# Last level of a blocked triangular inverse: 64x64 masked products against 32x32 blocks

## The reference, cut to what matters

```python
def rwkv7_scan(r, w, k, v, kk, a, s0):
    def step(s, inp):
        rt, wt, kt, vt, kkt, at = inp
        sa = jnp.einsum('nbhij,nbhj->nbhi', s, kkt)
        s = (s * wt[..., None, :] - sa[..., :, None] * (kkt * at)[..., None, :]
             + vt[..., :, None] * kt[..., None, :])
        return s, jnp.einsum('nbhij,nbhj->nbhi', s, rt)
```

## Time and profile before

| | us |
|---|---|
| median of 3 runs | 5243.85 |
| profiled execution | 5262.38 |
| its span | 5260.8 |
| stages ahead of the scans | 0 to 1540 |
| scans | 1540 to 3232 |
| readout, experts, combine | 3232 to 5261 |

### The profile page before, as it was taken

One profiled execution on the slowest core, in us unless ns is written; L12 is line 12 of the kernel. 1 busy time (PEld: TensorE's weight loads), 2 busy tenths in 40 slices (PEclk: granted clock), 3 DMA queues, 4 the chain that ended last, 5 costly groups with the idle time before them and its releaser, 6 DMA issues. The chain is left out here.

```text
span 5260.8 us, 122702 instructions
## 1 busy us (share of the span) xinstructions
PE 4374.7 (83%) x47298; PEld 2979.5 (57%) x47298; DVE 2214.8 (42%) x4008; ACT 1249.5 (24%) x3133; POOL 1565.5 (30%) x1949
## 2 busy tenths in 40 slices
PE   3998799989968988888888886788499999988990
PEld 1877676666648777777877775444133333333330
DVE  1112166666645454554544544888211111111118
ACT  0001044344423333333323332332000000000002
POOL 0000001001025464554545543443322222221224
PEclk7999999999989999999999988888699999999995
DMA  9311165556442223232232324442675888899766
GB/s 310 124 59 68 58 198 186 166 173 197 150 128 68 77 71 91 71 78 68 71 91 71 89 57 122 144 138 97 232 299 209 341 350 341 362 373 400 316 265 263
DMA packets 365528, 916.96 MB, mean 174 GB/s; under 512 B 181136, under 2 KB 220432, under 8 KB 332080
## 3 DMA queue, kind: packets, MB, share of 16 engines
q1 hardware_dynamic: 310224, 759.97, 41.4%
q0 software_dynamic: 47392, 133.02, 7.2%
q10 hardware_dynamic: 7488, 17.83, 0.9%
HBM read 951.09 MB, written 211.26 MB: 221 GB/s over the span
## 5 line engine op out<-in xcount | busy, mean ns | idle before, releaser
L2410 PE MATMUL exp_gate_up<-exp_w_gate,exp_rows_and_rowsT 128*64 128x512 f32 x1664 | 768.2, 620 | 88.8 <-DMA exp_w_up<-in_moe_w_up_dram 87.9
L2410 PE MATMUL exp_gate_up<-exp_w_up,exp_rows_and_rowsT 128*64 128x512 f32 x1664 | 768.9, 621 | 0.0
L2410 PEld LDWEIGHTS exp_gate_up<-exp_w_gate,exp_rows_and_rowsT 128*64 128x64 f32 x1664 | 234.9, 143 | 588.6 <-issue 588.6
L1544 POOL TENSOR_TENSOR rw_A_level<-rw_A_rho_beta,const_level_masks 128x256 f32<-128x256 f32 x432 | 338.2, 799 | 706.6 <-DVE rw_A_rho_beta L1560 440.0
L721 PE MATMUL rwp_product<-rwp_hT,rwp_w_rw 128*128 128x256 f32 (+1 forms) x2016 | 445.0, 384 | 0.0
L874 PE MATMUL hgp_product<-hgp_hT,const_w_hg 128*128 128x256 f32 x1728 | 411.1, 394 | 26.5 <-DMA hgp_hT<-s_hT 15.7
L2362 DVE TENSOR_TENSOR exp_hidden<-exp_hidden,exp_gate_up 64x512 f32<-64x512 f32 x104 | 71.9, 692 | 821.4 <-ACT exp_hidden L2343 821.4
L721 PEld LDWEIGHTS rwp_product<-rwp_hT,rwp_w_rw 128*128 128x128 f32 (+1 forms) x2016 | 381.7, 190 | 61.6
L874 PEld LDWEIGHTS hgp_product<-hgp_hT,const_w_hg 128*128 128x128 f32 x1728 | 338.0, 199 | 87.9 <-DMA hgp_hT<-s_hT 16.1
L2434 PE MATMUL exp_down<-exp_w_down,exp_hiddenT 128*64 128x512 f32 x1664 | 380.0, 598 | 1.1
L1575 DVE TENSOR_TENSOR rw_inverse<-rw_inverse,rw_inverse_bank 128x512 f32<-128x512 f32 x288 | 195.8, 684 | 349.6 <-PE rw_inverse_bank L1454 347.6
(11 more groups left out here) (384 smaller groups left out, 7977.6 us busy)
## 6 DMA issues: line engine op xcount, KB each, us to landing
exp_w_gate<-in_moe_w_gate_dram SPq DMA_DIRECT2D x104, 2048.0 KB
exp_w_up<-in_moe_w_up_dram SPq DMA_DIRECT2D x104, 2048.0 KB
exp_w_down<-in_moe_w_down_dram SPq DMA_DIRECT2D x104, 2048.0 KB
s_rw_in<-prep_operands SPq DMA_DIRECT2D x72, 514.0 KB, 4.0
rw_operands<-s_rw_in SPq DMA_DIRECT2D x72, 514.0 KB, 5.6
rw_tokens<-s_rw_tm SPq DMA_DIRECT2D x144, 192.0 KB, 6.5
hg_qkf<-s_hg_in SPq DMA_DIRECT2D x36, 768.0 KB, 7.9
mod_w<-in_w_mod_dram SPq DMA_DIRECT2D x24, 1024.0 KB, 26.1
```

The costliest lines, as they stand in the source:

```text
L1544: nc.gpsimd.tensor_tensor(self.al[d][l % 2][:], self.ar[u][d][:, :, 0, :], self.K["lvc"][:, d, l, :].unsqueeze(1).broadcast_to([P, NPAIR, ...
L2410: i = nc.tensor.matmul(pgu[u][q:q + BLK], xT[:, k, r * BLK:(r + 1) * BLK], w[r][:, k, :], start=(k == 0), stop=(k == KD - 1))
```

## The change

Level 5 joins the two diagonal blocks of 32. All that is new in the inverse is one block of 32x32 for each head, and its inputs are one block of 32x32 of the masked Gram product and the two diagonal blocks. For direction 0 the rows and columns 0 to 31 count as solved and 32 to 63 as the rest, for direction 1 the other way round (`halves`). After the change:
- cross5 multiplies 32x32 blocks, with the left operand taken from `rw_A_rho_beta` itself. It no longer waits for `level_ready`.
- ScalarE copies half of the columns of X at level 5 (all 128 partitions).
- grow5 multiplies 32x32 blocks.
- VectorE copies the new block into the inverse with two instructions of 32 partitions in place of the addition; one for each head of the pairs, the second with the semaphore.
- GpSimd makes no mask product for level 5. The counts of `level_ready` go from 6 to 5 a step, and the product of level 1 waits for cross3 of the step before, where it waited for cross5.

```diff
+    def halves(self, d):
+        early, late = slice(0, RW_C // 2), slice(RW_C // 2, RW_C)
+        return (early, late) if d == 0 else (late, early)
...
-            pe.wait_ge(s["level_ready"], 6 * n + l + 1)
+            if l < 5:
+                pe.wait_ge(s["level_ready"], 5 * n + l + 1)
             pe.sem_inc(self.turns, 1)
+            if l == 5:
+                solved, rest = self.halves(d)
+                for j in range(NPAIR):
+                    for h in (0, RW_C):
+                        i = nc.tensor.matmul(self.pa[d][at(rest, h), 0, j, solved], self.ar[u][d][at(solved, h), j, 0, rest],
+                                             self.rt[u][d][at(solved, h), 1, j, solved], start=True, stop=True)
+                i.then_inc(s["x_psum"], 1)
+                return
...
+            if l == 5:
+                solved, rest = self.halves(d)
+                for j in range(NPAIR):
+                    for h in (0, RW_C):
+                        i = nc.tensor.matmul(self.pa[d][at(solved, h), 0, j, rest], self.x[d][at(rest, h), j, solved],
+                                             self.rt[u][d][at(rest, h), 0, j, rest], start=True, stop=True)
+                i.then_inc(s["rd_psum"], 1)
+                return
...
-            nc.scalar.activation(self.x[d][:], self.pa[d][:, 0], ACT.Copy).then_inc(s["x_ready"], 1)
+            some = self.halves(d)[0] if l == 5 else slice(0, RW_C)
+            nc.scalar.activation(self.x[d][:, :, some], self.pa[d][:, 0, :, some], ACT.Copy).then_inc(s["x_ready"], 1)
...
-        for l in range(6):
+        for l in range(5):
...
-                    wait(pool, s["x_psum"], 5 * n + {0: -1, 1: 0, 3: 1, 4: 2, 5: 3}[l])
+                    wait(pool, s["x_psum"], 5 * n + {0: -1, 1: -2, 3: 1, 4: 2}[l])
...
-                    V.tensor_tensor(rt[:, 0], rt[:, 0], self.pa[d][:, 0], ALU.add).then_inc(s["r_ready"], 1)
+                    solved, rest = self.halves(d)
+                    V.tensor_copy(rt[solved, 0, :, rest], self.pa[d][solved, 0, :, rest])
+                    second = slice(RW_C + solved.start, RW_C + solved.stop)
+                    V.tensor_copy(rt[second, 0, :, rest], self.pa[d][second, 0, :, rest]).then_inc(s["r_ready"], 1)
```

More of the change, by code:

```diff
@@ L1449, in grow @@
             pe.sem_inc(self.turns, 1)
+            if l == 5:
[6 more added lines that the diff above has]
+                return
             for j, q in heads:
                 i = nc.tensor.matmul(self.pa[d][q, 0, j, :], self.x[d][q, j, :], self.rt[u][d][q, 0, j, :], start=True, stop=True)
-            if l < 5:
-                for j, q in heads:
-                    i = nc.tensor.matmul(self.pa[d][q, 1, j, :], self.rt[u][d][q, 0, j, :], self.x[d][q, j, :], start=True, stop=True)
+            for j, q in heads:
+                i = nc.tensor.matmul(self.pa[d][q, 1, j, :], self.rt[u][d][q, 0, j, :], self.x[d][q, j, :], start=True, stop=True)
             i.then_inc(s["rd_psum"], 1)
         chain = {"rhs": rhs, "solve": solve, "out": out, "state": state}
+        at = lambda part, h: slice(h + part.start, h + part.stop)
         if chain_only:
@@ L1532, in pool @@
         nc = self.nc
-        for l in range(6):
+        for l in range(5):
             for d in range(2):
                 s = self.s[d]
-                yield (({0: 3.1, 1: 5.1, 2: 7.1, 3: 10.1, 4: 16.1, 5: 22.1}[l] + d) / (2 * len(RW_ORDER)))
+                yield (({0: 3.1, 1: 5.1, 2: 7.1, 3: 10.1, 4: 16.1}[l] + d) / (2 * len(RW_ORDER)))
                 if l == 0:
@@ L1556, in mask @@
             if k == 0:
-                wait(dve, s["level_ready"], 6 * n)
+                wait(dve, s["level_ready"], 5 * n)
             wait(dve, s["y_psum"], n - 1)
@@ L1566, in inverse @@
             if l == 0:
-                dve.wait_ge(s["level_ready"], 6 * n + 1)
+                dve.wait_ge(s["level_ready"], 5 * n + 1)
                 wait(dve, s["u_psum"], n - 1)
```

## The result

The changed kernel takes 5361.55 us (median of 4 runs, 5355.20 to 5361.73), the one before on the same chip 5243.45 us (4 runs). The ratio is 1.0213, with an interval of 1.0176 to 1.0250: slower by 118 us. 5248 was forecast, with 5278 as the top of the range.

What follows compares the result with a forecast made beforehand. The scan stage was taken to go by TensorE's order of blocks plus 211 us idle. Long steps -8 and clock +12 gave +4 us: 5248, no change, own range 5238 to 5254; 8 in 10: 5226 to 5278.

Steps and rivals of the forecast that it cites:

- Block cost: A cross5 or grow5 block of one direction on TensorE: 0.26 us instead of 0.47, by the slope from 128 to 64 columns.
- The rival that blocks don't get shorter: 32 columns take the 29 ns of 64, leaving only idle edits, within 2 us of 5244; chance 0.10.
- Short steps: 18 scan steps ending in cross5, grow5, two HGRN blocks: no gain, 0.84 us saved only lengthens gram0's wait for loads.
- Long steps: 18 steps ending in cross5, grow5, score block, HGRN's output: three blocks save 0.63 us each step; 8 us taken.
- stops swallow half of the savings: TensorE's "issue" stops make half of the long steps lose their 0.63 us, leaving 5.7 of 11.3 us.
- Copies, X, relaxed wait: VectorE's two copies, ScalarE's half copy of X, GpSimd's earlier level 1 product: hidden behind other work or waits, 0.
- GpSimd's products: 72 level masks fewer on GpSimd, 57.5 us of its 872: 0, since no TensorE wait names them.
- The clock: Idle time between cross5 and grow5 in long steps drops TensorE to 1.2 GHz: +12 us, at 8 a stretch.
- the slower rival: Four more long steps fall to 1.2 GHz between cross5 and grow5, through HGRN's output: +24 us, 5268; chance 0.33.

Runs made afterwards that it cites:

- The copies alone: The kernel before with only VectorE's last addition replaced by two copies of the new block; ratio 1.0016.
- the stricter wait: The change with 64x64 blocks and GpSimd's level 1 product waiting again for cross5 of the step before; ratio 1.0070 to the kernel before.
- full tiles with 32 columns: The change with cross5 and grow5 as 64x64 tiles fed 32 columns each, four matmuls per direction and product; ratio 1.0189 to the kernel before.
- quarter tiles with 128 columns: The change with every 32x32 block of cross5 and grow5 fed 128 columns instead of 32; ratio 1.0124 to the kernel before.

## Why the prediction was wrong
**Block cost (0.26 us): right in size, not in its reason.** Measured 0.265. The rival that blocks don't get shorter falls. But the slope by columns, from which the 0.26 came, isn't what made them shorter: a 64x64 tile with half the columns isn't faster (1.13 against 1.15 us for 32 records), a 32x32 tile is. To that extent the number was luck. The Trainium skill gives a floor of about 25 ns from start to start ("TensorE: Matmul & The Clock Gate", Part 1). Counted by record, as the prediction did, the trace does not agree for the quarter tile, 0.53 us / 32 = 17 ns a record; the full tile's 35 ns lie above the floor. Counted by matmul, of which each leaves two records, both lie above it.

**Short steps (no gain): roughly right.** gram0's waits for loads were to grow from 31 to 45 us; they are 34.8. Short steps got 0.38 us shorter, so less of the 0.84 us went into these waits than was forecast.

**Long steps (-8): not seen.** The wait before cross5 of direction 1 grew from 0.82 to 0.92 us, where 1.0 was forecast. But the only long step of after without a long fall, the first one profiled, takes 51.20 us where the same step before takes 49.69; that is one step, with 3 us at the low clock. That stops swallow half of the savings has no run for or against it.

**Copies, X, relaxed wait (0): right.** The copies alone give 1.0016, the copies with the half copy of X and the product kept 1.0009, and the stricter wait gives nothing back. A copy takes 0.28 us (0.25 taken), X 0.28 us (0.38 before):

```profile
L1600 DVE COPY rw_inverse<-rw_inverse_bank 32x128 f32<-32x128 f32 x72 | 20.2, 280 | 72.9 <-PE rw_inverse_bank L1467 71.8
...
L1526 ACT ACTIVATE rw_X<-rw_inverse_bank 128x128 f32<-128x128 f32 x72 | 20.0, 278 | 108.6 <-PE rw_inverse_bank L1451 107.7
```

**GpSimd's products (0, "no wait on TensorE names it"): wrong.** Without them, and with the waits that go with them changed, the kernel is 0.5 per cent slower, some 25 us, with longer stops that the profile puts down to issue and some 25 us more at 1.2 GHz.

**The clock (+12): this step failed.** The place, the cause and the price of a fall were named, the sign was given (a stage clock of 0.93 or below; it is 0.87), and the slower rival is the mechanism that was shown. What failed is the count: "one or two further long stretches", four in the rival, where 16 of 17 long steps have a fall of 13.7 us or more and 3 had one before. 8 us a stretch was about right (6.6 by the estimate above). The count rested on one step with 2.58 us of work in 3.40 us that was held to have room, and on busy time: 0.2 us a block was taken out. The full tiles with 32 columns show that a block whose busy time is unchanged can lose the clock, so what the change took away isn't measured by its 0.84 us of busy time. By the measured sizes: 14.8 us more at 1.2 GHz in each of 17 long steps, at 0.89 / 2, cost 112 us, where 12 was taken.

## What to carry to other kernels
Before making matmuls smaller in front of a stretch that runs at the full clock, look at how near the clock's falls already are. Here 7 of 17 like steps fell at this place before, and all of them after; a few falls among like steps are a reason to put the whole number of such steps into the range, not one or two. Don't judge what is left in front of such a stretch by busy time alone: here two kernels with the same busy time there differed by 1.3 per cent. A saving at such a place cost about ten times itself (6.6 us a step, the estimate above, for the 0.63 us of three shorter blocks). And an experiment that added instructions to TensorE also added stops; widening a matmul did not.

## What the runs showed of the hardware
- Two blocks of 64x64 tiles took 1.13 us with 32 columns and 1.15 us with 64; 32x32 tiles took 0.53 us with 32 columns and 1.54 us with 128 (e.g. from 2252.89 to 2254.42 us, below).
- With the same instructions and busy time, and stops that were no longer, feeding the tiles 32 columns instead of 64 changed the time at 1.2 GHz from 8.1 to 15.3 us a long step, and from +26 to +226 us a run.
- Feeding the two blocks of cross5 in a long step twice the columns took 45 and 29 us off the time at 1.2 GHz in a run.
- Stops of TensorE that the profile puts down to "issue", some of them inside a block, rose from 70 us at three places (longest 3.3 us) to 134 us at five (longest 4.5 us) with 2,304 more matmul records (36 steps, 4 blocks of 16). The profile names no cause.
- Removing 72 GpSimd instructions that no wait of TensorE named, with the waits for them, cost 0.5 per cent.

```profile
2252.89 1.54 PE L1451 MATMUL rw_inverse_bank<-rw_inverse,rw_A_rho_beta 32*32 32x128 f32 x32
2254.42 1.54 PE L1467 MATMUL rw_inverse_bank<-rw_inverse,rw_X 32*32 32x128 f32 x32
```

The last two rows are from the quarter tiles with 128 columns, at the end of a short step.
